# Output and second input projections of a two-block model in wide pairs of matmuls, with later rounding of the raw tiles and narrower waits at three stage ends

## The reference

```python
# first block
h = rms_norm(x, mix_norm) @ w_in             # then three mixers and their gates
merged = sum(sigmoid(gate_b) * (y_b @ w_branch_b))
x = x + merged @ w_out                       # output projection 1: 2048 x 2048
x = x + conv_ffn(rms_norm(x, ffn_norm), w_up, ..., w_down)
x = rms_norm(x, final_norm)
# second block
proj = rms_norm(x, g_mix) @ w_in_2           # second input projection: 2048 x ...
...                                          # two attentions and their gates
x = x + (g0 * y_a + g1 * y_b) @ w_o          # output projection 2: 2048 x 2048
x = x + (silu(gate) * up) @ w_down_2         # gate, up = rms_norm(x, g_ffn) @ w_gate_up
```

## Time and profile before

| | |
|---|---|
| Time, median of 3 runs | 3098.6 us (3098.19 to 3101.96) |
| Profiled execution, its own time | 3111.46 us |
| Profiled execution, span first to last instruction | 3109.7 us |
| Mean granted clock of TensorE | 0.995 |
| PE busy | 3073.6 us |
| DVE busy | 1807.1 us |
| ACT busy | 1203.0 us |
| Weights and other data read | 526.94 MB |

### The profile page before, as it was taken

How to read it: one execution, slowest core, us unless ns; L and a number is a source line. 1 busy time by engine, 2 the same in 40 slices (tenths; PEclk the granted TensorE clock), 3 DMA queues, 4 the chain that set the end, 5 groups by cost and what they waited for, 6 DMA issues and landing times.

```text
span 3109.7 us, 47133 instructions
## 1 busy us (share of the span) xinstructions
PE 3073.6 (99%) x18712; PEld 2737.1 (88%) x18712; DVE 1807.1 (58%) x2356; ACT 1203.0 (39%) x1351; POOL 113.4 (4%) x80
## 2 busy tenths in 40 slices
PE   8999999999999999999999999999999999999999
PEld 8898898889998888888889977788999888888888
DVE  6673352867678888875555333322566666665444
ACT  5443102114444444444443312244445444444333
POOL 0000000000001100000000310000000000000000
PEclk9999999999999999999999999899999999999999
DMA  6554333445555555555555543223455555555555
GB/s 222 188 189 155 109 109 109 157 152 185 183 187 192 196 191 190 197 174 187 189 194 178 186 163 109 81 95 122 163 189 182 197 189 191 197 191 173 187 187 181
DMA packets 80147, 530.23 MB, mean 171 GB/s; under 512 B 9152, under 2 KB 9536, under 8 KB 27712
## 3 DMA queue, kind: packets, MB, share of 16 engines
q1 hardware_dynamic: 80064, 529.07, 49.7%
HBM read 526.94 MB, written 2.10 MB: 170 GB/s over the span
## 4 chain that ended last, share of the span: by engine, by line
PE 97%; DVE 1%; ACT 1%; issue 0%; DMA 0%; SPq 0%; ACTq 0%; DVEq 0%
PE bank L488 97%; DVE w_low L1461 0%; ACT w_high L1031 0%; DVE arena L1461 0%; PE bank L965 0%; DVE arena L1458 0%; DMA xT<-in_xT 0%; DVE arena L1491 0%; DVE xrs L1491 0%; DVE acts_both L1461 0%; DVE xtmp L1461 0%; ACT arena L1116 0%; ACT mix_high L1135 0%; DVE xT L1461 0%; ACT L1154 0%
## 5 line engine op out<-in xcount | busy, mean ns | idle before, releaser
L1461 DVE TENSOR_TENSOR w_low<-ring,w_high 128x2048 fp32r<-128x2048 f32 (+1 forms) x440 | 922.7, 2098 | 438.8 <-ACT w_high L1031 434.8
L1031 ACT ACTIVATE w_high<-ring 128x2048 fp32r<-128x2048 f32 (+1 forms) x448 | 787.4, 1759 | 472.4 <-DMA ring<-in_w_down 235.9
L488 PE MATMUL bank<-hT,ring 128*128 128x256 f32 x2560 | 569.2, 383 | 1.2 <-ACT arena L1378 1.2
L488 PEld LDWEIGHTS bank<-hT,ring 128*128 128x128 f32 x2560 | 488.1, 192 | 75.6 <-issue 7.3
L488 PE MATMUL bank<-acts_both,w_high 128*128 128x512 f32 x1408 | 492.9, 395 | 1.7 <-DVE arena L1461 1.3
L488 PE MATMUL bank<-up_early,w_high 128*128 128x512 f32 x1408 | 488.0, 389 | 1.3 <-issue 0.8
L488 PE MATMUL bank<-up_late,w_high 128*128 128x512 f32 x1408 | 487.3, 389 | 0.0
L488 PE MATMUL bank<-acts_both,w_low 128*128 128x256 f32 x1408 | 394.8, 280 | 0.0
L488 PE MATMUL bank<-up_early,w_low 128*128 128x256 f32 x1408 | 388.6, 276 | 0.0
L488 PE MATMUL bank<-up_late,w_low 128*128 128x256 f32 x1408 | 388.6, 276 | 0.0
L488 PEld LDWEIGHTS bank<-acts_both,w_high 128*128 128x128 f32 x1408 | 264.7, 188 | 63.1 <-issue 1.6
(11 more groups left out here) (277 smaller groups left out, 4084.8 us busy)
## 6 DMA issues: line engine op xcount, KB each, us to landing
ring<-in_w_up SPq DMA_DIRECT2D x176, 1024.0 KB, 4.8
ring<-in_w_down SPq DMA_DIRECT2D x128, 704.0 KB, 4.0
ring<-in_w_in SPq DMA_DIRECT2D x66, 1024.0 KB, 4.8
ring<-in_w_mix SPq DMA_DIRECT2D x62, 1024.0 KB, 4.8
ring<-in_w_gates SPq DMA_DIRECT2D x48, 1024.0 KB, 4.9
ring<-in_w_branch SPq DMA_DIRECT2D x16, 1024.0 KB, 4.8
ring<-in_w_out SPq DMA_DIRECT2D x16, 1024.0 KB, 4.8
ring<-in_w_o SPq DMA_DIRECT2D x16, 1024.0 KB, 4.8
```

The lines of the kernel that those rows point to most:

```text
L488: return nc.tensor.matmul(o, lhsT, rhs, start=first, stop=last)
L1031: A(w_high[:, s, 0:cols], ring[:, s, 0:cols], ACT.Copy).then_inc(rounded[s], 1)
L1461: return V.tensor_tensor(o, a, b, op)
```

## The change

Four things change. The high and low tiles of the output projections become one array (`out_both`, `out2_both`) and both output projections and the 26 feature units of the second input projection are done by `project_pairs`. DVE, which empties these banks, gets one more operation for each unit: in `residual_raw` two adds with a link between them, in the second input projection two multiplies and an add. In `round_raw` ACT rounds and squares tile n-1 after the weights of iteration n, and in `residual_raw` DVE lowers tile n-2 before the drain of unit n. The two `drained_all` after the output projections, the one before down 2, and the `down_drained` wait before the second input projection go; the last is put behind that projection's first unit, before the matmul of ones.

```diff
+        out_both = alias("out_both", arena_base, [P, 2, KT + 2, T], 28)
+        out2_both = alias("out2_both", arena_base, [P, 2, KT, T], 18)
+        out_high, out_low, out2_high, out2_low = out_both[:, 0], out_both[:, 1], out2_both[:, 0], out2_both[:, 1]
...
-            def merged_out(high, low):
+            def merged_out(both):
...
-                unit_split(project_split(high, low, waits))
+                pairs = [both[:, :, k] for k in range(KT)]
+                unit_split(project_pairs(pairs, waits))
                 for j in range(3):
-                    unit_split(project_split(high, low))
-                rounds_split(3, project_split(high, low))
+                    unit_split(project_pairs(pairs))
+                rounds_split(3, project_pairs(pairs))
...
                 pe.wait_ge(raw_summed, (KT - 1) * raws[0])
+                if second:
+                    for b in range(2):
+                        pe.wait_ge(down_drained[b], 1 + KT // 2)
                 mm(bank[4][:, 0], ones[:], xms[:]).then_inc(norm_summed, 1)
...
-            merged_out(each(out_high), each(out_low))
-            drained_all()
+            merged_out(out_both)
...
             down(0)
-            for b in range(2):
-                pe.wait_ge(down_drained[b], 1 + KT // 2)
-            raw_unit(lambda waits: project_split(in2_high, in2_low, waits), second=True)
-            unit_split(project_split(in2_high, in2_low))
-            rounds_split(2, project_split(in2_high, in2_low))
+            raw_unit(lambda waits: project_pairs(in2, waits), second=True)
+            unit_split(project_pairs(in2))
+            rounds_split(2, project_pairs(in2))
...
-            rounds_split(4, project_split(in2_high, in2_low))
+            rounds_split(4, project_pairs(in2))
...
-            merged_out(each(out2_high), each(out2_low))
-            drained_all()
+            merged_out(out2_both)
...
             rounds_split(21, project_pairs(ups))
-            drained_all()
             down(1)
...
+                def high(n):
                     s, _, _, _, free = units.next()
                     act.wait_ge(drained[s], free + 1)
                     A(ups[n][:, 0], xT[:, n], ACT.Copy, scale=v(gain, n)).then_inc(raw_rounded, 1)
-                    square_raw(n)
+
+                for n in range(KT):
+                    round_weights(UNIT)
+                    if n:
+                        high(n - 1)
+                        square_raw(n - 1)
+                high(KT - 1)
+                square_raw(KT - 1)
...
                     lower_weights(UNIT)
+                    if n > 1:
+                        low(n - 2)
+                        sum_raw(n - 2)
+                    if n == KT - 1:
+                        low(n - 1)
+                        sum_raw(n - 1)
                     dve.wait_ge(consumed[s], there)
-                    tt(xT[:, n], xT[:, n], bank[s][:, 0], ADD).then_inc(drained[s], 1)
-                    if n:
-                        lower_raw(n - 1, ups[n - 1][:, 0], ups[n - 1][:, 1], v(gain, n - 1))
-                        sum_raw(n - 1)
+                    link(tt(xT[:, n], xT[:, n], bank[s][:, 0], ADD))
+                    tt(xT[:, n], xT[:, n], bank[s][:, 1], ADD).then_inc(drained[s], 1)
...
+            dve.wait_ge(norm_done, norm[0])
...
-                tt(P2[:, u], bank[s][:, 0], xrs[:]).then_inc(drained[s], 1)
+                tt(P2[:, u], bank[s][:, 0], xrs[:])
+                tt(xtmp[:], bank[s][:, 1], xrs[:]).then_inc(drained[s], 1)
+                dve.wait_ge(drained[s], units.drained[s].value())
+                link(tt(P2[:, u], P2[:, u], xtmp[:], ADD))
```

More of the change, by code:

```diff
@@ L231, in build @@
         in2_high, in2_low = [x[:, 0] for x in in2], [x[:, 1] for x in in2]
-        out_high, out_low = (alias(f"out_{n}", arena_base, [P, KT, T], a) for n, a in (("high", 28), ("low", 46)))
-        out2_high, out2_low = (alias(f"out2_{n}", arena_base, [P, KT, T], a) for n, a in (("high", 18), ("low", 34)))
+        out_both = alias("out_both", arena_base, [P, 2, KT + 2, T], 28)
+        out2_both = alias("out2_both", arena_base, [P, 2, KT, T], 18)
+        out_high, out_low, out2_high, out2_low = out_both[:, 0], out_both[:, 1], out2_both[:, 0], out2_both[:, 1]
         y_high, y_low = alias("y_high", arena_base, [P, 12, T], 4), alias("y_low", arena_base, [P, M_TILES, T], 0)
@@ L1077, in round_raw @@
                 norm[0] += 1
-                for n in range(KT):
-                    round_weights(UNIT)
+                def high(n):
                     s, _, _, _, free = units.next()
@@ L1918, in residual_raw, with low @@
             def residual_raw(gain):
+                def low(n):
+                    lower_raw(n, ups[n][:, 0], ups[n][:, 1], v(gain, n))
                 for n in range(KT):
@@ L1922, in residual_raw @@
                     lower_weights(UNIT)
+                    if n > 1:
[4 more added lines that the diff above has]
+                        sum_raw(n - 1)
                     dve.wait_ge(consumed[s], there)
-                    tt(xT[:, n], xT[:, n], bank[s][:, 0], ADD).then_inc(drained[s], 1)
-                    if n:
-                        lower_raw(n - 1, ups[n - 1][:, 0], ups[n - 1][:, 1], v(gain, n - 1))
-                        sum_raw(n - 1)
+                    link(tt(xT[:, n], xT[:, n], bank[s][:, 0], ADD))
+                    tt(xT[:, n], xT[:, n], bank[s][:, 1], ADD).then_inc(drained[s], 1)
                     if n == KT - 1:
                         dve.wait_ge(drained[s], free + 1)
-                lower_raw(KT - 1, ups[KT - 1][:, 0], ups[KT - 1][:, 1], v(gain, KT - 1))
+                low(KT - 1)
                 sum_raw(KT - 1)
```

## The result

The kernel after takes 3087.4 us (median of 6 runs, 3082.57 to 3089.45), the kernel before on the same chip 3100.3 (6 runs, 3098.19 to 3108.78). The ratio is 0.9936, 95% interval 0.9914 to 0.9958: faster. The forecast was 3080.0 in 3073 to 3091.

A forecast was written before the change was run, and what follows sets the result against it. PE was taken as the bound, busy 3073.6 of 3109.7 us. Terms -1.5 - 1.8 - 1.6 - 7.1 - 6.6 = -18.6 us took the median of 3098.6 to 3080.0, range 3073 to 3091.

The forecast's parts named there:

- Output projections: Both output projections, 256 steps each: pairs at 350 ns instead of triples, -1.5 us for both, with -6.7 as other end.
- Feeding it: Output projections: with rounding one unit late and lowering two late, DVE and ACT stay hidden; the second add costs nothing.
- The ring of the old order: Output projections: drain, high tile, square, w_high, w_low, next drain; 5.77 us with the second add, over 5.45, setting the pace.
- Ends of the output projections: Gaps between output projections and up stages: without the stops, -1.0 and -0.8 us; tile 15's low part stays hidden.
- before down 2: Gap ahead of down 2: PE's stop of 1.50 us and 0.1 of restart go, -1.6 us.
- Down 2 at 340: Down 2: never stopped, it keeps 340 ns through its 704 pairs, -7.1 us; bounds 0 and -7.1.
- 350 after a stop: Down stages: pairs with high and low far apart keep 340 ns until something stops them, then run at 350.
- Second input projection: Second input projection: -2.4 us from the first four units, -4.6 from the other 22, +0.4 at the end; -6.6 together.
- The 22 units: Second input projection after its first four units: side by side operands run at 340.3 ns after a stop, -4.6 us.
- Output projections at 340 with down 2 at 340: Rival: output projections also run at 340 ns, beside down 2; -23.8 us, 3074.8 us; chance 0.16.
- Pairs are worth hardly anything: Rival: rounded steps stay at 350 ns everywhere new and in down 2; -7.9 us, 3090.7 us; chance 0.10.
- The up stages lose their cadence: Slower rival: up stages entered from 350 ns keep it; +16.9 us, 3115.5; chance 0.04 including another new wait.

The follow-up runs named there:

- the second session: The changed kernel run once more, unaltered, against the kernel before: 3089.4 us, ratio 0.9944.
- the moved norm: Kernel after with the second input projection's norm chain ahead of lowering the third unit's weights, fifth unit's after the first drain: 3081.2 us, ratio 0.9919 to before.

## Why the prediction was right, point by point

**The total.** Range and sign held. The forecast difference of 18.6 us is 0.60% of before; the ratio says 0.64%, with the second session 0.56%, the medians of this one 0.41%. The point of 3080 lay 7.4 us low. 1.7 of this is the base: six runs of before have a median of 3100.3 where three had 3098.6. The rest comes of a step that no term shows: the 18.6 us were worked out on an execution of 3111.46 us, whose down stages ran at 350 but for 21 pairs, and taken off a median 12.9 us below it. Going by the times, some of those shorter runs had a down stage at 340 already, and nothing more to gain there; they weren't traced. And the agreement of the sum is in part luck: two terms were wrong by 5.3 and 5.4 us in opposite directions.

**Output projections (forecast -1.5, measured -6.8).** A mis-sized term. Operands 18 and 16 tiles apart ran at 339.6 ns, not at the 350 taken; the other end of the bounds, -6.7, was right. The choice rested on reading 350 as a property of operands that lie apart. It isn't: one execution had output projection 2 and another output projection 1 at 350 (89.48 us), and both cadences occur with each kind of operand. What made `ups` look safe is something else, which the traces show and the prediction didn't see. Two executions entered up 2 at 350, one out of an output projection at 350 and one out of the stop of the wait put back. Both kept 350 through the first unit and were at 340 behind the matmul of ones that follows it, without a stop. PE in the first of them, the pairs' first matmuls 15 pairs apart on either side of the ones (5.25 us, then 5.10):

```profile
2366.71 0.40 PE L489 MATMUL bank<-up_early,w_high 128*128 128x512 f32 x1
...
2371.96 0.40 PE L489 MATMUL bank<-up_late,w_high 128*128 128x512 f32 x1
...
2372.31 0.59 PE L489 MATMUL bank<-xms,ones 128*128 128x256 f32 x2
...
2373.44 0.39 PE L489 MATMUL bank<-up_early,w_high 128*128 128x512 f32 x1
...
2378.54 0.39 PE L489 MATMUL bank<-up_early,w_high 128*128 128x512 f32 x1
```

Undoing the pairs gave 90.33 us back.

**Feeding it.** Right in the size, wrong in the place. The ring of the old order is 5.77 us. But it didn't set PE's pace inside the stage, as was said: the lateness of 4 us came out as waits in the up stage, and in the traced execution the reorder was worth more than its arithmetic, since that stage then ran at 350 behind its stop.

**Ends of the output projections (-1.0, -0.8) and before down 2 (-1.6).** Right: the gaps went from 1.05, 0.79 and 1.61 us to 0.11 or 0.12, and came back with the waits. Tile 15 was in time, as was the third unit's `w_low` of down 2.

**Down 2 at 340 (-7.1).** Right for the two executions compared, and too large over the runs. "350 after a stop" was the failed step. Of four executions with the stop ahead of down 2 three ran it at 350 (246.38 us) and one at 340; of ten without the stop all ran it at 340. Down 1, whose stop of 0.33 us the change keeps, also comes out both ways: behind that stop 350 in five executions and 340 in seven, and 6.8 us of the table belong to that. No term of the prediction had them. Whether the change makes 340 likelier there, by the wait that it takes from in front of up 1, is open (see the waits put back). In the kernel before the prediction could have seen it only in a second execution.

**Second input projection (-6.6, measured -1.2 in the table, -2.3 with the second execution of after).** Two steps failed. First, the norm chain doesn't move with PE's start. It begins 8.2 us after the last matmul of down 1 (9.1 before), as it stands behind DVE's low weights, which wait for ACT; the chain itself is 18.3 us as it was. So the fifth unit starts 27.4 us after down 1's end where it started 27.9, and the 2.6 us of the earlier start became a stop: 4.47 us, not 2.5. The row with "1.08 <-PE bank" was read as the rule for the chain's start; its releaser was simply the last of two that were 1 us apart. Second, a stop of that length was priced at its length. Behind it the clock was granted at 0.50 and some 2.6 us more went. The 22 units weren't all at 340 either: in this execution they ran at 350 from 1634.8 to 1665.5, which is 0.9 us.

**The rivals.** Output projections at 340 with down 2 at 340 came true in the traces (3074.8 was its time, 12.6 us below the median, by the base and the step from the traced execution told above). "Pairs are worth hardly anything" fell: a step saves (90.33 - 86.93) / 256 = 13.3 ns, 3.4 us a stage. By the formula in the Trainium skill, "TensorE: Matmul & The Clock Gate", section "Back-to-back issue gap", which that section gives for isolated matmuls and the prediction used for a stream, a pair would save 2.5 ns, an estimated 0.6 us a stage; the trace doesn't agree. "The up stages lose their cadence" was priced on a path that the traces refute: entered at 350, the up stages of three executions were at 340 in their second unit. One of 28 up stages traced did run at 350, in the kernel with the old order and behind a stop in its fourth unit, and cost 16.4 us where the rival had 14.2 for one stage.

**Still open.** What draws 340 or 350. To 350 it went mostly at a stop; two output projections were at 350 straight from the triples ahead of them, with no stop between. Back to 340 it went, without a stop, in each of the eight places where a stream at 350 met a few matmuls of another kind: the ones behind the first unit of an up stage (2) or of the second input projection (2), and four small ones ahead of that projection's eleventh unit (4). No stream at 340 came out of such a place at 350. The down stages have no such matmuls, and one that was entered at 350 kept it for all 704 pairs. That is what goes together in the traces; no run adds or removes such a matmul, so the cause isn't shown. And why the clock falls to 0.93 or 0.90 in the attention part of some executions.

## What to carry to other kernels

A wait that is taken from one engine only pays in full if the chain that ends the next wait starts with it: look for what stands ahead of the chain's first operation on its own queue, and move that. The stop of 4.47 us cost some 2.6 us more than its length, and the one of 0.41 us that the moved norm left cost no clock, so shortening such a stop can pay more than its length. And when two stages with the same instructions differ by 3%, trace the same kernel twice before building a term on it: here 7 us a stage came and went with the execution. A difference read from one execution is taken off that execution's time; off the median of others it may count a gain twice.

## What was unexpected of the hardware

- The same stream of a 512 and a 256 column matmul with full granted clock has two cadences, 340 and 350 ns (239.24 and 246.38 us for 704 pairs), stable over hundreds of pairs. Triples of 256 columns have 353 ns in each execution.
- A stream at 350 was at 340 again behind a few matmuls of another kind, in eight cases of eight and without a stop.
- The granted clock fell to half behind stops of 2.49, 2.70, 2.80, 3.09 and 4.19 to 4.65 us, and the unit behind such a stop took 1.3 to 2.7 us more. It also fell behind a stop of 1.78 us that had a wait of 0.4 us close behind it (the old order, up 2). It didn't behind the stop of 2.44 us in the kernel before, whose window right after it is this:

```profile
1616.30:1620.00 3.70, 3.65 (x31) 3.68 (x32) 1.82 (x4) 3.68 (x5) 0.00 (x0) 1.00 0.55 228
```

- Feeding the stage ahead faster can bring this on: with down 1 at 340 the wait for its last drains was 2.70 and 2.80 us, with down 1 at 350 it was 2.39 to 2.44.
